# The end of a two-layer trunk on one core: gate weight in the picking tile, an identity matmul for the residual, statistics from the bank, output in four transfers

## The reference, cut to what matters

```
def moe_swiglu(x, router, w_gate, w_up, w_down):
    logits = (x @ router).astype(jnp.float32)
    top_vals, top_idx = lax.top_k(logits, TOP_K)          # TOP_K = 2
    gates = jax.nn.softmax(top_vals, axis=-1)
    combine = jnp.sum(jax.nn.one_hot(top_idx, N_EXPERTS) * gates[..., None], axis=-2)
    y = jnp.zeros_like(x)
    for e in range(N_EXPERTS):                            # 8 experts, D_EXPERT = 3584
        y = y + combine[..., e:e + 1] * swiglu(x, w_gate[e], w_up[e], w_down[e])
    return y
# and at the end of the layer:
h = layer_norm(ALPHA * h + ffn, ln_g[i, 2], ln_b[i, 2])   # (h - mean) * rsqrt(var + eps) * g + b
```

## Time and profile before

| | us |
|---|---|
| three runs | 1654.07, 1654.28, 1656.89; median 1654.28 |
| the profiled execution, its own time | 1653.97 |
| its span, first to last instruction | 1652.0 |
| PE busy in the span | 1605.9 (97%) |
| DVE busy | 1269.3 (77%) |
| ACT busy | 1035.8 (63%) |
| last matmul of the weight stream starts | 1637.28 |
| last instruction of DVE ends | 1648.91 |

### The profile page before, as it was taken

One profiled execution on the slowest core, in us unless ns is written; L12 is line 12 of the kernel. 1 busy time (PEld: TensorE's weight loads), 2 busy tenths in 40 slices (PEclk: granted clock), 3 DMA queues, 4 the chain that ended last, 5 costly groups with the idle time before them and its releaser, 6 DMA issues.

```text
span 1652.0 us, 21357 instructions
## 1 busy us (share of the span) xinstructions
PE 1605.9 (97%) x7602; PEld 1321.5 (80%) x7602; DVE 1269.3 (77%) x1188; ACT 1035.8 (63%) x935; POOL 118.3 (7%) x129
## 2 busy tenths in 40 slices
PE   8999999999999999999999999999999999999997
PEld 7777878888787687788888888888888888888775
DVE  5687565454746676789889889888888988988996
ACT  4464544443445543668777777777777777777673
POOL 2102010000113201000000000000000000000120
PEclk9999999999999999899999999999999999999999
DMA  9537655466455462899999999999999999999992
GB/s 334 177 103 234 225 171 186 130 224 208 154 193 177 143 221 72 290 373 362 389 378 376 388 366 386 389 362 388 389 359 383 388 369 385 388 358 390 361 362 99
DMA packets 238104, 480.11 MB, mean 291 GB/s; under 512 B 8224, under 2 KB 11328, under 8 KB 238048
## 3 DMA queue, kind: packets, MB, share of 16 engines
q1 hardware_dynamic: 229744, 454.06, 76.9%
q0 software_dynamic: 6288, 21.63, 4.1%
q10 hardware_dynamic: 2016, 3.67, 0.6%
HBM read 473.54 MB, written 11.03 MB: 293 GB/s over the span
## 4 chain that ended last, share of the span: by engine, by line
PE 84%; DVE 7%; issue 5%; DMA 3%; ACT 1%; POOL 1%; DVEq 0%; SPq 0%; POOLq 0%; ACTq 0%
PE bank L379 26%; PE bank L381 26%; PE bank L380 26%; DMA c_add<-gate_rows 2%; PE bank L845 1%; DVE w_lo L1944 1%; PE bank L423 1%; PE bank L666 1%; PE bank L644 1%; DVE w_lo L1456 1%; DVE X L1493 1%; DVE X L1502 1%; POOL c_add L926 1%; DMA raw<-in_ab_w_in_dram 0%; DVE stats L1482 0%
## 5 line engine op out<-in xcount | busy, mean ns | idle before, releaser
L1088 ACT ACTIVATE w_hi<-raw 128x2048 fp32r<-128x2048 f32 (+1 forms) x322 | 608.7, 1895 | 231.8 <-PE bank L381 222.5
L1944 DVE TENSOR_TENSOR w_lo<-raw,w_hi 128x2048 fp32r<-128x2048 f32 x221 | 503.1, 2290 | 81.8 <-ACT w_hi L1088 78.5
L1456 DVE TENSOR_TENSOR w_lo<-raw,w_hi 128x2048 fp32r<-128x2048 f32 (+1 forms) x96 | 211.2, 2205 | 135.3 <-ACT w_hi L1088 135.2
L379 PE MATMUL bank<-w_hi,xe_hi 128*128 128x512 f32 x736 | 293.0, 398 | 1.5 <-DVE w_lo L1944 1.5
L381 PE MATMUL bank<-w_hi,xe_lo 128*128 128x512 f32 x736 | 288.0, 391 | 0.0
L380 PE MATMUL bank<-w_lo,xe_hi 128*128 128x512 f32 x736 | 287.2, 390 | 0.0
L379 PE MATMUL bank<-w_hi,xT_hi 128*128 128x512 f32 (+1 forms) x560 | 218.1, 390 | 3.6 <-DVE w_lo L1456 3.4
L380 PE MATMUL bank<-w_lo,xT_hi 128*128 128x512 f32 (+1 forms) x560 | 214.1, 382 | 0.0
L381 PE MATMUL bank<-w_hi,xT_lo 128*128 128x512 f32 (+1 forms) x560 | 214.0, 382 | 0.0
L381 PEld LDWEIGHTS bank<-w_hi,xe_lo 128*128 128x128 f32 x736 | 138.4, 188 | 29.9
L379 PEld LDWEIGHTS bank<-w_hi,xe_hi 128*128 128x128 f32 x736 | 138.7, 188 | 29.1 <-DVE w_lo L1944 1.9
(11 more groups left out here) (281 smaller groups left out, 2150.8 us busy)
## 6 DMA issues: line engine op xcount, KB each, us to landing
raw<-in_moe_w_gate_dram SPq DMA_DIRECT2D x96, 1024.0 KB, 9.0
raw<-in_moe_w_up_dram SPq DMA_DIRECT2D x96, 1024.0 KB, 8.3
raw<-in_moe_w_down_dram SPq DMA_DIRECT2D x96, 1024.0 KB, 7.0
raw<-in_mem_wkv_dram SPq DMA_DIRECT2D x16, 1024.0 KB, 5.0
raw_more<-in_moe_w_up_dram SPq DMA_DIRECT2D x16, 1024.0 KB, 8.6
raw_more<-in_moe_w_gate_dram SPq DMA_DIRECT2D x16, 1024.0 KB, 8.6
raw_more<-in_moe_w_down_dram SPq DMA_DIRECT2D x16, 1024.0 KB, 7.4
raw<-in_c_w_in_dram SPq DMA_DIRECT2D x12, 1024.0 KB, 5.0
```

What stands on the lines that cost most here:

```text
L379: nc.tensor.matmul(d, xh, hi[:, k, :], start=(first and k == 0), stop=False)
L1088: return nc.scalar.activation(dst, src, ACT.Copy)
L1456: tt(w_lo[s][:, 0:n], raw[c % NRAW][:, 0:n], w_hi[s][:, 0:n].bitcast(F32), ALU.subtract).then_inc(lo_made, 1)
L1944: tt(w_lo[s][:, :], raw_exp[r][:, :], w_hi[s][:, :].bitcast(F32), ALU.subtract).then_inc(lo_made, 1)
```

## The change

In the last job alone, and behind it:

- The turn of `pick` on PE moves from c = 4 to c = C_TURN = 32, and DVE's copy to `pickT` from c = 5 to c = 33. In between, at c = 6, DVE multiplies `pick` by the gate weight `w_fin[:, 2, t]` (two instructions of 128 x 128), so that `pickT` holds the weight and `combine` gives the weighted sum.
- The left half is then added by a plain `tensor_tensor`.
- For the right half PE first puts X itself into the two banks, by a matmul with the identity, and adds `combine` to it; DVE no longer adds. It takes `bn_stats` out of the bank, and (bank - mean) * g straight out of the bank too.
- The chain from `bn_stats` to the reciprocal is done for each block by itself, and ACT takes two roots instead of one.
- Centring and scaling go in halves of 512 columns, and the output leaves in four transfers of 256 KB instead of two of 512 KB.

```
             def combine(half, job):
+                d = [claim(pe, f"c{half}{t}", 2 * half + t, job) for t in range(TB)]
+                if half:
+                    pe.wait_ge(sem("y_added"), 2 * TB)
+                    for t in range(TB):
+                        nc.tensor.matmul(d[t][:, :], ident[:, :], X[:, t, W:2 * W], start=True, stop=False,
+                                         skip_group_check=True)
+                pe.wait_ge(sem(f"y_made{half}"), job + 1)
                 for t in range(TB):
-                    d = claim(pe, f"c{half}{t}", 2 * half + t, job)
-                    if t == 0:
-                        pe.wait_ge(sem(f"y_made{half}"), job + 1)
-                    nc.tensor.matmul(d[:, :], pickT[...], y[...], start=True, stop=True, ...)
+                    nc.tensor.matmul(d[t][:, :], pickT[...], y[...], start=(half == 0), stop=True, ...)
                         .then_inc(filled[2 * half + t], 1)
...
-                    if c == C_INDEX:
+                    if c == C_INDEX and not z:
                         pe.wait_ge(sem("picked"), job + 2)
-                        if z:
-                            (pT claimed, pick transposed twice)
-                        else:
-                            index("iB", job)
+                        index("iB", job)
+                    if c == C_TURN and z:
+                        pe.wait_ge(sem("pick_scaled"), 1)
+                        (pT claimed, pick transposed twice)
...
             for t in range(TB):
-                sp.wait_ge(sem("out_made"), t + 1)
-                sp.dma_start(out[0]...[:, t, :], X[:, t, :]).then_inc(sem("out_done"), 16)
+                for half in range(2):
+                    c = slice(half * W, (half + 1) * W)
+                    sp.wait_ge(sem("out_made"), TB * t + half + 1)
+                    sp.dma_start(out_rows[:, t, c], X[:, t, c]).then_inc(sem("out_done"), 16)
...
             preload(ACT.Sqrt)
-            act.wait_ge(sem("vars_made"), 1)
-            nc.scalar.activation(rstd[:, :], rstd[:, :], ACT.Sqrt).then_inc(sem("rstds_made"), 1)
+            for t in range(TB):
+                act.wait_ge(sem("vars_made"), t + 1)
+                nc.scalar.activation(rstd[:, t:t + 1], rstd[:, t:t + 1], ACT.Sqrt)\
+                    .then_inc(sem("rstds_made"), 1)
...
                 link(tt(w_fin[:, 2, :], w_fin[:, 0, :], w_fin[:, 1, :], ALU.add))
+                for t in range(TB):
+                    ins = nc.vector.tensor_scalar(pick[:, t, :], pick[:, t, :], w_fin[:, 2, t:t + 1], None,
+                                                  ALU.mult)
+                ins.then_inc(sem("pick_scaled"), 1)
...
-            add_last(1, last)
-            for t in range(TB):
-                ins = nc.vector.bn_aggr(mean_var[:, t, :], ...)
-            link(ins)
-            link(nc.vector.tensor_scalar(var_eps[:, :], mean_var[:, :, 1], LN_EPS, None, ALU.add))
-            nc.vector.reciprocal(rstd[:, :], var_eps[:, :]).then_inc(sem("vars_made"), 1)
...
+            def variance(t):
+                b = wait_filled(dve, f"c1{t}", last)
+                link(nc.vector.bn_stats(stats[:, t, 1, :], b[:, :]))
+                nc.vector.bn_aggr(mean_var[:, t, :], ...).then_inc(sem("means_made"), 1)
+                dve.wait_ge(sem("means_made"), t + 1)
+                v = var_eps[:, t:t + 1]
+                link(nc.vector.tensor_scalar(v, mean_var[:, t, 1:2], LN_EPS, None, ALU.add))
+                nc.vector.reciprocal(rstd[:, t:t + 1], v).then_inc(sem("vars_made"), 1)
+
+            def centred(t):
+                nc.vector.scalar_tensor_tensor(out=X[:, t, 0:W], in0=X[:, t, 0:W], ...)
                 return nc.vector.scalar_tensor_tensor(
-                    out=X[:, t, :], in0=X[:, t, :], scalar=mean_var[:, t, 0:1], in1=gb[:, 0, :], ...)
-            centre(0)
-            dve.wait_ge(sem("rstds_made"), 1)
+                    out=X[:, t, W:2 * W], in0=bank_of(f"c1{t}")[:, :], ..., in1=gb[:, 0, W:2 * W], ...)
+            variance(0)
+            variance(1)
+            centred(0)
+            dve.wait_ge(sem("rstds_made"), TB)
             (Newton step as before)
             for t in range(TB):
                 if t:
-                    link(centre(t))
-                nc.vector.scalar_tensor_tensor(out=X[:, t, :], in0=X[:, t, :], scalar=rstd[:, t:t + 1], ...)
+                    link(centred(t))
+                for half in range(2):
+                    c = slice(half * W, (half + 1) * W)
+                    nc.vector.scalar_tensor_tensor(out=X[:, t, c], in0=X[:, t, c], scalar=rstd[:, t:t + 1], ...)
                         .then_inc(sem("out_made"), 1)
```

More of the change, by code:

```diff
@@ L794, in combine @@
             def combine(half, job):
-                for t in range(TB):
-                    d = claim(pe, f"c{half}{t}", 2 * half + t, job)
-                    if t == 0:
-                        pe.wait_ge(sem(f"y_made{half}"), job + 1)
-                    nc.tensor.matmul(d[:, :], pickT[:, t * P:(t + 1) * P], y[:, half * W:(half + 1) * W],
-                                     start=True, stop=True, skip_group_check=True)\
+                d = [claim(pe, f"c{half}{t}", 2 * half + t, job) for t in range(TB)]
[5 more added lines that the diff above has]
+                pe.wait_ge(sem(f"y_made{half}"), job + 1)
+                for t in range(TB):
+                    nc.tensor.matmul(d[t][:, :], pickT[:, t * P:(t + 1) * P], y[:, half * W:(half + 1) * W],
+                                     start=(half == 0), stop=True, skip_group_check=True)\
                         .then_inc(filled[2 * half + t], 1)
@@ L1915, in add_got, with add_last @@
                 nc.vector.nop().then_inc(sem("y_added"), 1)
-            def add_last(half, job):
+            def add_last(job):
                 for t in range(TB):
-                    xs = X[:, t, half * W:(half + 1) * W]
-                    b = wait_filled(dve, f"c{half}{t}", job)
-                    link(nc.vector.scalar_tensor_tensor(
-                        out=xs, in0=b[:, :], scalar=w_fin[:, 2, t:t + 1], in1=xs,
-                        op0=ALU.mult, op1=ALU.add))
-                    ins = nc.vector.bn_stats(stats[:, t, half, :], xs)
+                    xs = X[:, t, 0:W]
+                    b = wait_filled(dve, f"c0{t}", job)
+                    link(tt(xs, b[:, :], xs, ALU.add))
+                    ins = nc.vector.bn_stats(stats[:, t, 0, :], xs)
                 link(ins)
@@ L1977, in expert @@
                     if z and c == C_COMBINE + 1:
-                        add_last(0, job)
+                        add_last(job)
             with dve.Fori(0, last) as job:
```

32 lines of the change are left out of this document (16 added, 16 removed).

## The result

| | before | changed |
|---|---|---|
| median (20 runs of each, alternating) | 1653.96 us | 1657.42 us |
| lowest and highest | 1650.48, 1658.10 | 1653.59, 1658.46 |
| ratio to before, 95% interval | | 1.0017 [1.0011, 1.0023] |
| the profiled execution | 1653.97 | 1655.80 |
| its span | 1652.0 | 1653.8 |

The ratio says 2.8 us slower, 1.8 to 3.8; the two medians lie 3.5 apart. I had said 1653.8, a little faster, and a range up to 1656.3. The prediction is wrong in sign and in size. Only its coarse statement holds: 0.91 for a change of less than 3.3 us either way. The 0.04 for slower was for more than that.

The account below looks back on a forecast made before the run. PE was taken as the bound while weights stream, then one chain through ACT, `combine`, DVE and the last transfer. Inside -0.12 and behind the stream -0.39 summed to -0.51 us: median 1653.8, range 1651.9 to 1656.3.

Parts of the forecast that it names:

- The step that failed: Last expert, DVE's copy at step 33: 0.93 us of idle time hides its 0.74, so it costs nothing.
- the case for "faster": Whole kernel: faster by more than 3.3 us, needing the clock's gain with every lower bound; chance 0.05.
- PE's wait for `e_h` at 1541: Last expert, PE waiting for DVE: shrinks from 2.08 to 1.73 us because `e_h` comes 0.35 us earlier.
- inside, S1: From chunk 8's split start on DVE to chunk 28's: `e_h` 0.35 us earlier, passed on through the gathers; bounds 0.1 and 0.6.
- stream's end to DVE's first row: Behind the weight stream: identity pair takes 1.72 us, 1.02 hidden behind ACT's copy of `y`, +0.70 exposed.
- DVE's rows at the end: DVE's work behind the stream: 9.25 us becomes 8.81, so -0.44; bounds -0.9 and +0.2.
- last row of DVE to the span's end: Output: last transfer of 256 KB instead of 512 KB ends 0.65 us sooner; bounds 0 and -0.9.
- behind the stream together, S3: From the weight stream's end on PE to the span's end: +0.70 - 0.44 - 0.65 = -0.39 us.
- The clock's rival: Behind PE's shorter `e_h` wait the clock may stay up; if PE's lost 1.70 us were on the path, 1652.1; chance 0.13.
- The identity pair in full: Behind the stream: the pair costs 1.72 us instead of 0.70, giving 1654.8; chance 0.15.
- the small pieces: Kernel's end: 256 KB transfers end no sooner and DVE needs what it needed, giving 1654.9; chance 0.12.
- The rule weighed: DVE's four bank reads on the path: skill's table adds an estimated 0.26 us, giving 1654.1; prediction kept 1653.8.

Follow-up runs that it names:

- e2: Kernel before with only the late turn of `pick` (before chunk 32) and its copy at step 33: median 1657.57 us, ratio 1.0017.
- e5: Changed kernel with the turned `pick` in bank 7 instead of bank 5, turn and copy left in place: median 1652.58 us, ratio 0.9997.
- e9: Changed kernel with DVE's copy of the turned `pick` one step earlier, at step 32: median 1653.47 us, ratio 1.0002.
- e6: Changed kernel with DVE's copy of the turned `pick` one step later, at step 34: median 1662.10 us, ratio 1.0057.
- e4: Kernel before with only the last scaling in halves and the output in four transfers of 256 KB: median 1654.23 us, ratio 1.0001.
- e8: Kernel before with only the turn of `pick` before chunk 28 and its copy at step 30: median 1652.65 us, ratio 1.0000.
- e1: Changed kernel with the turn of `pick` before chunk 28 and its copy at step 30: median 1652.00 us, ratio 0.9992.
- e7: e1 without the identity matmuls, DVE adding the right half of X instead: median 1653.44 us, ratio 1.0001.
- e3: e1 with the identity matmul and `combine` taken block by block: median 1652.54 us, ratio 0.9990.
- e10: Changed kernel run once more, unedited, on the same chip as e9: median 1657.60 us, ratio 1.0027.

## Why the prediction was wrong, point by point

**The step that failed** is this one: "The copy at step 33 stands behind the split of chunk 37. There DVE has 0.93 us of idle time for `w_hi`, which hides 0.74." All of it was true of DVE's time, and the changed kernel bears it out: the next split still waits 0.84 us for its `w_hi`. But I asked only who waits for what stands *behind* the copy, and the answer, chunk 38's split, has slack. I did not ask who waits for the copy itself. I named `combine` only as what stands ahead of PE's need for chunk 38, and never the bank that the copy empties, though the code says that the turned `pick` lies in bank 5 and that the two halves of the down product accumulate in banks 4 and 5. The question to put is: which instruction of PE writes bank 5 next, and does PE get there before the copy? The rows on record would have answered it. `combine` of the left half starts at 1625.02, behind chunk 37, so chunk 35 starts three chunks of 12 matmuls of 0.227 us earlier, at 1616.85, or 1617.1 with the turn ahead of it. DVE ends the split of chunk 37 and begins its idle time at 1619.71 - 0.93 = 1618.78: the copy starts 1.7 us after PE has come to chunk 35, and with the 0.70 from the copy's start to the matmul's, seen afterwards, that makes 2.4. The wait cost 2.43 where the term had 0. e2 shows the loss with this edit alone, e5 takes it away by the bank alone, and e9, the changed kernel and e6 give the wait as a function of the copy's place: between the starts of the two matmuls 0.23 us over the usual at step 32, 2.43 at 33, 5.89 at 34.

**What I said would show me wrong** did not name it either: "if `w_lo` becomes late behind step 33". The last clause, "if the stream ends over 1 us away from 1637.6", did catch it: it ended at 1639.83. One sum of mine was wrong besides, without effect here: the case for "faster" leaves out the turn's +0.23 and takes the identity pair as -0.2 where its lower bound is +0.5, so that every lower bound together makes -3.4 and not the -4.3 of its terms.

**The other terms**, predicted and measured:

| term | predicted | measured |
|---|---|---|
| PE's wait for `e_h` at 1541 | 2.08 to 1.73 | 1.72 |
| turn on PE at step 32 | +0.23 | +0.23 (1607.66 to 1608.35 is 0.69, two matmuls 0.46) |
| inside, S1 | -0.35 | -0.60 and -0.13 in two profiles |
| wait for bank 5 | 0 | +2.43, +0.10 behind it |
| stream's end to DVE's first row | +0.70 | +0.74 (1642.55 - 1639.83 = 2.72, before 1.98) |
| DVE's rows at the end | -0.44 | -0.51 (1651.29 - 1642.55 = 8.74, before 9.25) |
| last row of DVE to the span's end | -0.65 | -0.58 (2.51, before 3.09) |
| behind the stream together, S3 | -0.39 | -0.33 |

*The multiplications of `pick`* took what two of that size had taken in the earlier trace rows, in the changed kernel's timeline:

```profile
1538.54 0.48 DVE L1913 TENSOR_SCALAR pick<-pick,w_fin 128x128 f32<-128x128 f32 x2
...
1541.12 0.65 PE L849 MATMUL bank<-ident,e_h 128*128 128x128 f32 x4 [1.72 <-DVE e_h L1947]
```

*The clock's rival* was half right. Behind that shorter wait the granted clock stayed at 1.00, as the window that answers to the first of the earlier trace rows shows, and yet PE got little of the 1.70, as I argued: it stood at 1584.04 for 1.96 us instead of 1.45, and from 1541 to its wait at 1596 it took 55.13 us instead of 55.37.

```profile
1542.50:1545.90 3.40, 3.40 (x16) 2.79 (x15) 3.40 (x3) 1.33 (x1) 0.00 (x0) 1.00 0.69 203
```
```profile
1570.23 3.01 POOL L1064 DMA_INDIRECT y_got<-y_rows,row_i  x1 [7.22 <-DVEq L1927]
...
1580.72 0.75 DVE L1924 SCALAR_TENSOR_TENSOR X<-y_got,g,X 128x512 f32<-128x512 f32 x1 [1.53 <-DMA y_got<-y_rows,row_i]
...
1584.04 0.50 PE L379 MATMUL bank<-w_hi,xe_hi 128*128 128x512 f32 x1 [1.96 <-DVE w_lo L1954]
```

The chain is the one of the earlier trace rows: gathers, DVE, split, PE. It does pass DVE's savings on. From the start of chunk 8's split to the first of the sums (`add_got`) DVE takes 26.43 us before and 26.42 in e4, and 25.79 to 25.81 in the other ten profiles, 0.63 less. That is the 0.35 that I forecast and 0.28 behind `e_h`, which goes with the clock: with PE at full speed DVE no longer waits for `w_hi` at 1548. I had that at under 0.2. e2 and e8, without the multiplications of `pick`, gain no more than the others: there `e_h` waits for ACT's `e_g`, which I had not looked at. The 0.39 for the multiplications was the right duration and cost nothing.

Behind that the gathers' own time decides. From POOL's issue to DVE's second sum, the second and the third pair together took 21.75 us in e1, 21.84 in the changed kernel, 21.92 in e7, 22.05 in e3, 22.42 in e10, 22.54 in e6 and 22.64 in e2 (before 21.92). S1 of these seven goes with them, from 63.55 to 64.44, and is 41.80 to 41.92 more than that sum in each. And PE's wait at 1584, longer now because PE arrives earlier, is itself one behind which the clock fell in e5, e8 and e9: there S1 is 42.53 to 42.60 more than the gathers' time, so the fall cost 0.74 us. The changed kernel's two profiles, -0.60 and -0.13, lie within my bounds of 0.1 and 0.6. e1 with -0.81 and e6 with -0.02, which have the same instructions up to there, do not: the bounds were too narrow for what the gathers do.

*The identity pair in full, and the small pieces*, my two slower rivals, did not happen: PE went from the pair straight into `combine` (1641.55 in the chain), and the transfers gained most of what I gave them. The rival I lacked was a wait that takes the place of the one removed, on a resource rather than a result.

*The rule weighed.* The lines of the changed kernel behind 1640 (total us, mean ns) put the reads from a bank beside those from a tile:

```profile
L2009 DVE SCALAR_TENSOR_TENSOR X<-bank,mean_var,gb 128x512 f32<-128x512 f32 x2 | 1.5, 744 | 0.0
L2006 DVE SCALAR_TENSOR_TENSOR X<-X,mean_var,gb 128x512 f32<-128x512 f32 x2 | 1.5, 738 | 0.0
```

The bank costs 6 ns more, from start to start some 10 (0.65 and 0.66 us in the chain above), and `bn_stats` from the bank took 688 ns where it took 0.69 us from a tile before. The Trainium skill, "VectorE: DVE Perf Modes", section on the TRN2 errata, would have 62 cycles more per read, an estimated 65 ns each; this trace does not bear it out for these two operations.

**The size beyond the profile is open.** S1 to S3 give -0.60 + 2.81 - 0.33 = 1.9 us, the profiled execution is 1.8 slower; the ratio says 2.8, and between e10 and e9, one line apart and on the same chip, the medians differ by 4.1 us where S2 differs by 2.2. I supposed, in the expectations of e2 and e10, that in part of the executions the clock falls behind the wait of 2.27. e6 shows that it can, behind a longer wait, and that it then costs 2.3. In the three profiles with the 2.27 (the changed kernel, e2, e10) it did not. The mean granted clock, which is on record for every execution, does point to the clock: it averages 0.99035 in the 37 executions of the changed kernel, e2 and e10, and 0.99162 in 68 of e1, e3, e5, e7, e8 and e9 (all but the one of 5402.73 us). Of 1653 us that difference is an estimated 2.1 us of full clock, near what the profiles leave unexplained. But where in the kernel it falls the profiles do not show, so the excess is measured and its cause is not shown. My range was too narrow besides: a kernel whose executions spread over 5 to 8 us needs more room than half the spread of three runs.

## What to carry to other kernels

When an instruction is moved later, list everything that it releases, and the buffer or bank that it empties above all, and then find the next writer of that bank on the engine that bounds the kernel; idle time on the engine where it stands hides its duration, not its lateness. In an in-order list one place can decide: the copy behind chunk 36's split held PE up for 0.2 us, behind chunk 37's for 2.4 us, behind chunk 38's for 5.9. A step may be moved freely only between the point where its input is ready and the one where the bound engine needs its buffer back, and a bank without a near second use (e5) widens that window at no cost that S2 shows. The end of the kernel itself did gain, by S3 0.33 us as changed and 0.71 when taken block by block (e3); that is what is left to use once the turn stands early enough.

## What the runs showed of the hardware

Whether the granted clock falls behind a wait of PE was not settled by the wait's length. It fell behind 2.00 us (e8), 2.07 (e4), 2.08 (before), 2.17 (e9), 2.20 (e5) and 5.74 (e6), each time to 0.50, and it stayed at 1.00 behind 2.03 (e3), 2.26 and 2.27 (e10, the changed kernel), 2.28 (e6), 2.32 (e2) and 2.42 (e10, at 1585). In e6 it was 0.50 from 1618.6 on, while PE was still waiting. What a fall costs depends on what else holds PE: 0.74 us of S1 at 1583, 2.3 us behind the wait for the bank in e6.

In the changed kernel, e2, e6 and e10 PE's wait for the bank shows as a wait for "DVEq" and the line of an empty instruction, not as one for the copy, and in e9 the 0.23 us that is left shows as no wait at all. The distance to read is from the copy's start to the matmul's: 0.70 us in the changed kernel, e2, e6 and e9 alike, 0.42 of it the copy.
